# A hybrid decoder layer on one core: q and k of all gated-delta heads projected first, one triangular solve for twelve blocks, and the norm's row factor applied behind the projections

## The reference

```
h = rms_norm(x, norm_w)                      # x * rsqrt(mean(x*x) + eps) * norm_w
proj = h @ w_in                              # 2048 -> 4*(4+6+6)*128 + 12 columns
# 4 retention heads, 6 gated-delta heads, 6 block-attention heads, 128 wide
# gated-delta group, per head, in chunks:
q, k, v = silu(causal_conv4(proj_q)), silu(causal_conv4(proj_k)), silu(causal_conv4(proj_v))
q, k = l2_norm(q) * 128**-0.5, l2_norm(k)
g, beta = -exp(a_log) * softplus(a + dt_bias), sigmoid(b)
decay = exp(g_cum[i] - g_cum[j]);  m = strict_lower((k*beta) @ k.T * decay)
w, u = triangular_solve(m + I, [k*beta*exp(g_cum), v*beta])
v_new = u - w @ state;  o = (q*exp(g_cum)) @ state + (q @ k.T * decay) @ v_new
y = rms_norm(o, gdn_norm_w) * silu(z)
out = x + concat(y_ret, y_gdn, y_moba) @ w_out
```

## Time and profile before

| | before |
|---|---|
| median of 3 runs | 545.01 us (544.94 to 545.31) |
| profiled execution: time, span of its instructions | 544.99 us, 543.2 us |
| PE busy, PE weight loads | 529.7 us, 443.8 us |
| DVE, ACT, POOL busy | 326.8, 276.8, 47.4 us |
| granted TensorE clock over the span | 0.999 |
| chain that ended last | PE 96%, DMA 1%, ACT 1% |

### The profile page before, as it was taken

The page is one execution under the profiler, slowest core; times in us unless marked ns, Lnnn a source line. Parts: engine busy times, 40 slices in busy tenths (PEclk is TensorE's granted clock), DMA queues, the critical chain, the costliest instruction groups (busy, mean ns, idle before and its releaser), DMA issues.

```text
span 543.2 us, 8033 instructions
## 1 busy us (share of the span) xinstructions
PE 529.7 (98%) x3104; PEld 443.8 (82%) x3104; DVE 326.8 (60%) x548; ACT 276.8 (51%) x439; POOL 47.4 (9%) x49
## 2 busy tenths in 40 slices
PE   3999999999999999999999999999999999999997
PEld 3887888888888887788888888888888888888885
DVE  2776877768687877556454545366455445646451
ACT  4766664556455653446553554555366446543330
POOL 1003030212031021100100000010010001000000
PEclk9999999999999999999999999999999999999999
DMA  8997664546345653657567756765755666767811
GB/s 275 215 284 195 161 183 122 152 122 158 102 130 135 175 139 99 158 151 194 127 183 195 192 150 189 187 174 156 192 149 157 198 195 180 210 197 227 272 40 39
DMA packets 149929, 91.77 MB, mean 169 GB/s; under 512 B 7843, under 2 KB 139138, under 8 KB 149762
## 3 DMA queue, kind: packets, MB, share of 16 engines
q1 hardware_dynamic: 148562, 88.95, 60.7%
q10 hardware_dynamic: 1328, 2.31, 1.2%
HBM read 89.13 MB, written 2.10 MB: 168 GB/s over the span
## 4 chain that ended last, share of the span: by engine, by line
PE 96%; DMA 1%; ACT 1%; POOL 0%; issue 0%; DVE 0%; ACTq 0%
PE pj L1245 19%; PE pj L1243 19%; PE pj L1246 19%; PE pj L1221 13%; PE pj L1222 6%; PE pj L1287 3%; PE mx L1386 2%; PE mx L1376 2%; DMA cst<-table_dram 1%; PE pj L1292 1%; PE mx L1363 1%; PE pj L1218 1%; PE mx L1277 1%; PE mx L1270 1%; PE pj L1217 1%; PE mx L1460 1%
## 5 line engine op out<-in xcount | busy, mean ns | idle before, releaser
L292 DVE TENSOR_TENSOR w_lo<-w_raw,w_hi 128x1024 fp32r<-128x1024 f32 x160 | 194.6, 1225 | 90.9 <-ACT w_hi L374 90.7
L374 ACT ACTIVATE w_hi<-w_raw 128x1024 fp32r<-128x1024 f32 x160 | 169.1, 1058 | 152.1 <-PE pj L1246 136.4
L1243 PE MATMUL pj<-w_hi,hT 128*128 128x512 f32 x320 | 127.0, 397 | 0.0
L1245 PE MATMUL pj<-w_hi,hT 128*128 128x512 f32 x320 | 127.0, 397 | 0.0
L1246 PE MATMUL pj<-w_lo,hT 128*128 128x512 f32 x320 | 125.0, 391 | 0.0
L1221 PE MATMUL pj<-hT,w_hi 128*128 128x512 f32 x300 | 111.6, 408 | 0.0
L1222 PE MATMUL pj<-hT,w_lo 128*128 128x256 f32 x300 | 84.1, 280 | 0.0
L1246 PEld LDWEIGHTS pj<-w_lo,hT 128*128 128x128 f32 x320 | 60.1, 188 | 12.1
L1245 PEld LDWEIGHTS pj<-w_hi,hT 128*128 128x128 f32 x320 | 60.2, 188 | 12.0
L1243 PEld LDWEIGHTS pj<-w_hi,hT 128*128 128x128 f32 x320 | 60.1, 188 | 12.0
L1221 PEld LDWEIGHTS pj<-hT,w_hi 128*128 128x128 f32 x300 | 56.4, 188 | 12.0
(11 more groups left out here) (220 smaller groups left out, 487.5 us busy)
## 6 DMA issues: line engine op xcount, KB each, us to landing
w_raw<-in_w_in_dram SPq DMA_DIRECT2D x256, 256.0 KB, 3.4
w_raw<-in_w_out_dram SPq DMA_DIRECT2D x64, 256.0 KB, 4.0
big<-in_x_dram SPq DMA_DIRECT2D x8, 256.0 KB, 5.4
out_dram<-sq ACTq DMA_DIRECT2D x8, 256.0 KB, 4.1
big<-in_x_dram SPq DMA_DIRECT2D x1, 1024.0 KB, 4.9
big<-in_x_dram SPq DMA_DIRECT2D x2, 512.0 KB, 7.6
cst<-table_dram SPq DMA_DIRECT2D x1, 682.0 KB, 5.9
cst<-table_dram ACTq DMA_DIRECT2D x1, 196.0 KB, 7.4
```

What stands on the lines that cost most here:

```text
L292: eng.tensor_tensor(w_lo[:, n % NSPLIT, :], w_raw[:, n % NRAW, :], w_hi[:, n % NSPLIT, :].bitcast(F32), ALU.subtract).then_inc(S("lo"), 1)
L374: act.activation(w_hi[:, n % NSPLIT, :], w_raw[:, n % NRAW, :], ACT.Copy).then_inc(S("hi_done"), 1)
L1243: ins = pe.matmul(bank[:, :], src[:, kc, 0, tok], hi[:, k, :], start=first, stop=False)
L1245: pe.matmul(bank[:, :], src[:, kc, 1, tok], hi[:, k, :], start=False, stop=False)
```

## The change

1. **Start.** x is loaded in five column pieces of 2, 2, 4, 4 and 4 blocks, the pieces laid between the weight tiles in SP's queue. The identity alone (`cst[:, 0:P]`) is the first DMA of ACT's queue. x is transposed unscaled; group 0 needs the norm's weight but not its row factor. Squares are summed in quarters behind the blocks, the row factor is ready near the end of group 0, is spread by two transposes into `rb` (128 x 256), and multiplies the results: POOL's `add_halves` has a second operation per section, DVE multiplies the a/b rows, and ACT's copies of groups 6 to 15 take it as their scale. The small parameter DMAs move from SP's queue into ACT's.
2. **Order of columns.** `section(g, s)` makes groups 0 to 2 the q and k of heads pairs 0, 1, 2, and groups 3 to 5 their v and z.
3. **Solve.** `prepare(j)` (Gram, norms, decay, k rows) of the three pairs stands at units 110 to 262; then all 12 blocks are solved as one, 16 units a level; then `chain(p)` of the three pairs, 32 units each, ends before unit 512. Intermediates lie in the not yet written half of `yT` (`home`). The solve's matmuls are the same in number and shape.

```diff
-HALVES = [(0, 0), (2, HALF), (1, 0), (3, HALF), (0, HALF), (2, 0), (1, HALF), (3, 0)]
+HALVES = [(n + m, (a + m * HALF // GDN) % P) for a in (0, HALF) for n in range(GDN) for m in (0, GDN)]
...
+U_SUM, U_CUM = 74, 100
+U_ROWS = (110, 150, 200)
+U_PREP = (120, 176, 240)
+U_SOLVE = 262
+U_X = [U_SOLVE + 16 * _l for _l in range(LEVELS - 1)]
+U_Y = [_u + 7 for _u in U_X]
+U_VTOK, U_TURN = U_Y[3], U_Y[4] + 9
+U_X[5], U_Y[5] = U_TURN + 4, U_TURN + 11
+U_CHAIN = [U_Y[5] + 7 + 32 * _j for _j in range(GDN // 2)]
...
+        X_PIECES = [(0, 2), (2, 4), (4, 8), (8, 12), (12, 16)]
...
             for n in range(TILES):
                 load(n)
+                if n in (0, 1, 3, 5):
+                    load_piece(sp, (n + 1) // 2 + 1)
...
-            act.dma_start(cst[:, 0:K_FIRST], table[:, 0:K_FIRST]).then_inc(S("cst_in"), 16)
+            act.dma_start(cst[:, 0:P], table[:, 0:P]).then_inc(S("ident_in"), 16)
+            act.dma_start(prow[R_NORM:R_CONV, :], norm_w[0].rearrange("(k p) -> k p", p=P)).then_inc(S("ident_in"), 16)
...
-                pool.tensor_tensor(raw[:, g % 2, s, PAD:], ev[:, n % 2, 0:T], ev[:, n % 2, T:2 * T], ALU.add).then_inc(S("evac"), 1)
+                pool.tensor_tensor(ev[:, n % 2, 0:T], ev[:, n % 2, 0:T], ev[:, n % 2, T:2 * T], ALU.add).then_inc(S("halves"), 1)
+                if n == 0:
+                    pool.wait_ge(S("rb_done"), 1)
+                pool.wait_ge(S("halves"), n + 1)
+                pool.tensor_tensor(raw[:, g % 2, s, PAD:], ev[:, n % 2, 0:T], rb[:, :], ALU.mult).then_inc(S("evac"), 1)
...
-            pe.wait_ge(S("cst_in"), 16)
-            pe.wait_ge(S("norm_in"), 16)
+            pe.wait_ge(S("ident_in"), 2 * 16)
             pe.transpose(mx[3][:, 0:KC], prow[0:KC, :], ident[0:KC, 0:KC]).then_inc(S("norm_psum"), 1)
-            keep_busy(14)
-            pe.wait_ge(S("x0_scaled"), 1)
+            keep_busy(3)
             for b in range(2):
-                x_blocks(b, 0)
-            keep_busy(6)
-            pe.wait_ge(S("x1_scaled"), 1)
-            for b in range(2):
-                x_blocks(b, 1).then_inc(S("hT_psum"), 1)
-            keep_busy(8)
+                pe.wait_ge(S(f"x_in{b}"), 16 * C)
+                for c in range(C):
+                    ins = x_blocks(b, c)
+                ins.then_inc(S("hT_psum"), 1)
+                keep_busy(4)
...
+            pe.wait_ge(S("rstd_done"), 1)
+            for c in range(C):
+                pe.transpose(mx[3][:, c * P:(c + 1) * P], sm[:, 6 + c:7 + c].broadcast_to([P, P]), ident)
...
-            stream(68)
+            stream(U_SUM)
...
+            silu_kq(0, 0)
+            advance(106)
+            silu_kq(0, 1)
+            advance(112)
             decay_clip(0)
+            advance(116)
+            conv(1, 0, 0)
             decay_mask(0)
+            advance(122)
+            conv(1, 1, 0)
+            advance(128)
+            norms(0)
...
+            solve()
```

More of the change, by code:

```diff
@@ L303, in _ @@
         def _(sp):
[L304 to L307, removed]
+            load_piece(sp, 0)
             def load(n):
@@ L849, in _ @@
             dve.wait_ge(S("cst_in2"), 16)
-            for sec in range(3):
-                conv(0, 0, sec)
             steps = [0]
@@ L1020, in mix_gdn @@
+                    advance(U_X[l - 1] + 5)
                     if l == 1:
[L1021 to L1031 removed]
@@ new lines, in _ @@
+            conv(1, 1, 0)
+            advance(128)
+            norms(0)
+            advance(136)
+            conv(1, 0, 1)
+            advance(142)
+            lower(0)
+            scalars(0)
+            advance(148)
+            inverse_of_pairs(0)
+            queries(0)
+            advance(154)
+            conv(1, 1, 1)
+            decay_clip(1)
+            advance(160)
+            silu_kq(1, 0)
+            silu_kq(1, 1)
+            decay_mask(1)
+            advance(168)
+            conv(2, 0, 0)
@@ new lines, in _ @@
+            advance(176)
+            conv(2, 1, 0)
+            advance(184)
+            norms(1)
+            advance(192)
+            conv(2, 0, 1)
+            advance(200)
+            lower(1)
+            scalars(1)
+            advance(206)
+            inverse_of_pairs(1)
+            queries(1)
+            decay_clip(2)
+            advance(212)
+            conv(2, 1, 1)
+            silu_kq(2, 0)
+            advance(222)
+            silu_kq(2, 1)
+            decay_mask(2)
+            advance(236)
@@ new lines, in _ @@
+            norms(2)
+            advance(242)
+            lower(2)
+            inverse_of_pairs(2)
+            advance(248)
+            queries(2)
+            solve()
+            for p, (kind, j) in enumerate(PAIRS):
+                if kind == "gdn":
+                    chain(p)
+                else:
+                    if PAIRS[p - 1][0] == "gdn":
+                        mean_square(p - 1, True)
+                        norm_out(p - 1, True)
+                        advance(U_CHAIN[p - 1] + 38)
+                        gated_pair(p - 1, mx[2], [sm[:, 96 + RET:97 + RET]] * 2)
+                    {"ret": mix_ret, "moba": mix_moba}[kind](p, j, 128 * (p + 1))
@@ L1364, in mix_gdn @@
                                         start=True, stop=True)
                 ins.then_inc(S("gram"), 1)
+                pe.wait_ge(S("sq"), 2 * j + 2)
+                pe.wait_ge(S("clip_done"), 4 * j + 4)
+                for h in range(2):
+                    pe.transpose(mx[3][:, h * P:(h + 1) * P], kqs[:, j, h, 0, 0, :], ident)
+                for n in range(4):
+                    ins = pe.matmul(mx[3][:, 2 * P + n:2 * P + n + 1], sq[:, n // 2, n % 2, 1, :], ones[:, 0:1], start=True, stop=True)
@@ L1366, in mix_gdn, with v_tokens, solve @@
+                ins.then_inc(S("ktr"), 1)
+            def v_tokens(j):
+                pe.wait_ge(S("silu_v"), j + 1)
+                if j:
+                    pe.wait_ge(S("os"), j)
+                for n in range(4):
+                    ins = pe.transpose(mx[2][:, n * P:(n + 1) * P], vT[:, n // 2, (n % 2) * P:(n % 2 + 1) * P], ident)
+                ins.then_inc(S("vtok"), 1)
+            def solve():
                 for l in range(1, LEVELS):
-                    stream(U[f"x{l}"])
+                    stream(U_X[l - 1])
```

805 lines of the change are left out of this document (408 added, 397 removed).

## The result

The changed kernel takes 539.44 us in the median of four runs (537.86 to 540.47) against 544.98 (544.67 to 545.31): a ratio of 0.9898, 95% interval 0.9878 to 0.9917. Forecast were 535.3, with a range of 531 to 541.5. It is faster, inside the range, and 4.1 us short of the forecast.

The account below looks back on a forecast made before the run. PE bound the kernel, busy 529.7 of 543.2 us. From 544.99: -7.2 start, -0.6 a/b wait, +0.3 row-factor transposes, -7.0 merged batches, +3.6 DVE late, +1.2 POOL beside DVE, giving 535.3 us; range 531 to 541.5.

Parts of the forecast that it names:

- The start: Before group 0: PE starts earlier, group 0 begins at 8.3 instead of 15.49, gain 7.2 us; row-factor transposes later cost 0.3.
- about 6 us, before PE asks for them: Initial loads: identity, first x pieces and tile 0 arrive by about 6 us, so PE does not wait for x's second piece.
- double behind 3.4 us of transposes: Transposes before group 0: PE's pace doubles after 3.4 us of transposes alone, as read from the trace before.
- rival C: Start and first tile: transposes don't raise PE's pace, so group 0 begins slow, costing 2.3 us, 537.6 us; chance 0.12.
- The a/b wait: After group 0: PE's wait for the copy of the a/b rows goes, since ten units stand before the use; -0.6 us.
- The merged batches: Solve on PE: a 48-matmul batch costs 1.80 us, three of 16 cost 2.40; saving the fixed part gives -7.0 us.
- DVE late, and POOL beside it: Unit 64 to 262: DVE's list ends late, +3.6 us; twelve more POOL operations slow DVE, +1.2 us.
- Most are cheap: POOL beside DVE before unit 262: conv's mean lies just 17 ns above its median, so each added operation costs DVE 0.1 us.
- between nothing and 0.37: POOL beside DVE before unit 262: bounds in us of DVE's loss per added POOL operation, 0 to 4.4 us in all.
- the four places: Where PE stalls on DVE: decay rows 0.9, k rows of pair 0 0.5, Gram of pair 1 1.1, solve start 0.8 us.
- the distances between steps are those of before: Chains after the solve: step distances unchanged, so no waits or costs were counted there.
- rival D: Merged solve: DVE's widened steps make PE wait at each of twelve steps, slower than before, 550.9 us; chance 0.04.

Follow-up runs that it names:

- repaired: Changed kernel with dummy matmuls after x block 0 doubled, row-factor transposes after 4 gate-column matmuls, retention out batches 4 units later: 537.17 us, ratio 0.9853.
- start_only: Kernel before with only the change's new start, own order of heads and 16-matmul batches kept, no merged solve: 545.53 us, ratio 1.0011.
- low_parts_early: Changed kernel with DVE's low parts of tiles 9 and 10 done before its wait for the a/b projection: 539.86 us.
- taps_two: Changed kernel with one of DVE's three conv steps left out (18 conv steps fewer in the trace), POOL's work kept: 534.54 us.
- start_only_2: Kernel before with only the new start, no merged solve, decay-sum batch at unit 98 and first row batch at 106: 549.34 us.
- row_mult_twice: Changed kernel with each POOL multiply by the row factor made twice, 24 more POOL instructions, same results: 545.34 us, ratio 1.0005 to the kernel before.
- late_solve: Changed kernel with decay rows, preparation and solve placed 4 to 14 units later: 539.40 us.
- solve_in_thirds: Changed kernel with each of the twelve merged solve batches cut on PE into three parts, one stream unit apart: 546.33 us.
- no_row_mult: Changed kernel without POOL's 24 multiplies by the row factor (groups 0 to 5 left unscaled): 535.53 us, ratio 0.9829.
- start_only_3: Kernel before with only the new start, no merged solve, convs spread between gate steps, gate sums at unit 72, first rows at 102: 543.89 us, ratio 0.9984.

## Why the prediction was right or wrong

The forecast was a gain of 9.7 us, the measured one 5.5; the range held. Between the forecast and the profiled execution lie 5.2 us, 1.0 of which is this execution's distance from the median.

**The start** was the largest error in this execution: -6.9 forecast with the row factor's transposes, -4.5 measured at unit 64. Three steps failed. The first is the order of "about 6 us, before PE asks for them": x's second piece came after PE was ready, a gap of 0.66 us, and group 0 began at 8.89 and not 8.3.

The second is the pace. The prediction has it double behind 3.4 us of transposes; but the x block at 11.84 in the kernel before still ran at the slow one (1.06 us for four), and the distances halve at about 12.95, 4.4 us behind PE's first instruction. Here they halve at about 11.2, in the first tile, 7.4 us behind PE's first instruction, which costs 1.1. This is rival C, in part: the tile is slow, at half of its 2.3. What delays the doubling stays open. Counted from PE's first instruction it came after 4.0 us in *repaired*, with no gap, and after 7.4 and 7.5 with gaps of 0.66 and 0.82. But in between there is no order: a gap of 0.3 gave a first tile of 2.09 in *start_only*, 2.46 in *low_parts_early* and 2.95 in *taps_two*, and one of 0.6 gave 2.12 in *start_only_2* and 2.90 in *row_mult_twice*. One execution without a gap doesn't show that the gap is the cause. The rule that rival C named ("TensorE: Matmul & The Clock Gate", Part 4, of the Trainium skill) would have the first tile slow in either kernel; the fence of *repaired*, where the pace doubles among the transposes (0.60 us for the last four), speaks against it, as the earlier trace rows did.

The third was not foreseen at all: PE waits 0.6 us for the row factor. POOL's power takes 1.81 us where it takes 0.70 in *repaired*, *late_solve* and three more runs: it starts 0.02 us before a low part of DVE and stands still behind it. Nothing between 0.70 and 1.80 occurs in the eleven executions with this start, six long and five short, and only the long ones leave PE waiting, so this term too is a matter of chance.

**The a/b wait** went, as forecast: -0.65.

**The merged batches** were right in mechanism and near in size: -8.4 by the trace, -6.9 by *solve_in_thirds*, -7.0 forecast. A 48-batch cost 1.74, not 1.80. The fixed part of a batch is what merging saves, 0.29 to 0.35 us.

**DVE late, and POOL beside it**: +3.6 and +1.2 forecast, 4.8 together; to the start of the solve the three stalls cost 1.6, 1.6 and 1.5 between starts of PE, 4.7. But the split was wrong. Without the multiplies one stall of 1.1 is left there, so the load alone makes about 1, and the contention 3.9 and not 1.2. "Most are cheap" is the sentence that failed: a multiply cost DVE 0.29 us in the mean (7.0 / 24 by *no_row_mult*), not 0.1, near the upper end of the prediction's own "between nothing and 0.37". The earlier trace rows show the adds where DVE had slack, and the changed kernel has two POOL instructions per section where DVE has none. And of the four places two came (decay rows; Gram of pair 1), the k rows and the start of the solve did not, and a low part at 111.1 took the place of the latter. That the sum came out, 4.8 against 4.7, was luck.

**After the solve** nothing was counted ("the distances between steps are those of before"). The out transposes lost 2.6 us: where the batches of all eight pairs should take 0.45 us each, 3.6, they took 6.2. About half of that lies in the chains of the gated-delta heads (at 201.4 and at 231.1, with the wait of 0.7), half in the two retention pairs (0.4 of wait each). *repaired* gives the retention pairs 4 units more, and their two waits are gone; the one at the gated-delta chain it leaves as it was.

In the solve itself the 12-block steps of DVE took 0.95 to 0.98 us, as forecast, and PE waited for none: rival D had nothing. Adding up by the starts of PE: -4.5 for the start, -0.65 - 8.4 + 7.3 behind it (4.7 + 2.6), together -6.25 where the span fell by 4.8. That leaves some 1.5 us spread over the execution that I could not place, and 0.3 outside the span.

The net by parts, from medians: the start alone 1.1 (*start_only_3*), the merge 6.9 (*solve_in_thirds*), together 8.0, and the change gave 5.5. The 2.5 between them agree in size with the out transposes' 2.6, but no run isolates that, and the two parts were measured in kernels with different orders of columns.

## What to carry to other kernels

An engine with no waits in front of it makes each head start of the bottleneck a loan: ask, for every microsecond won early, whether the second engine can deliver that much earlier too. Small batches between the instructions of a saturated PE cost a fixed part each, so merge them, once the widened steps of the other engine fit the gaps. When an instruction is added to POOL, count what stands on DVE at that moment, not POOL's own idle time; here each cost DVE 0.29 us in the mean. And before two executions are compared, see whether their starts differ by chance: here one and the same start code put unit 64 anywhere between 37.9 and 39.8 us.

## What the runs showed of the hardware

**A POOL instruction waits for a whole DVE instruction.** Same stretch of the changed kernel, two engines in one timeline:

```profile
40.57 3.08 POOL L781 TENSOR_TENSOR ev<-ev 128x256 f32<-128x256 f32 x1
...
40.71 2.34 DVE L326 TENSOR_TENSOR w_lo<-w_raw,w_hi 128x1024 fp32r<-128x1024 f32 x2
```

3.08 is 0.74, the duration with DVE idle, and 2.34, both low parts. A power of four columns shows it too, with DVE idle and with a low part of 1.23 us that starts at 267.00:

```profile
229.07 1.01 POOL L754 TENSOR_TENSOR sm<-sm,cst 128x4 f32<-128x4 f32 x1 [7.47 <-DVE sm L974]
267.09 2.01 POOL L754 TENSOR_TENSOR sm<-sm,cst 128x4 f32<-128x4 f32 x1 [30.73 <-DVE sm L976]
```

So the two don't share a rate, one stands still, and DVE's conv steps of up to 1.02 us instead of 0.48 beside POOL are the same thing the other way round. Who goes first can turn on very little. The power of the row factor and a low part start 0.02 to 0.03 us apart in the changed kernel and in *late_solve*:

```profile
33.92 1.81 POOL L754 TENSOR_TENSOR sm<-sm,cst 128x2 f32<-128x2 f32 x1 [33.06 <-DVE sm L875]
33.94 1.22 DVE L326 TENSOR_TENSOR w_lo<-w_raw,w_hi 128x1024 fp32r<-128x1024 f32 x1
```

```profile
32.97 0.70 POOL L754 TENSOR_TENSOR sm<-sm,cst 128x2 f32<-128x2 f32 x1 [32.12 <-DVE sm L875]
33.00 1.25 DVE L326 TENSOR_TENSOR w_lo<-w_raw,w_hi 128x1024 fp32r<-128x1024 f32 x1
```

In the second the low part loses 0.03 us and the power nothing; in the first the power loses 1.1 and PE behind it 0.6. The recorded starts don't tell who goes first: POOL's is the earlier in both, and also in the add at 40.57 that waits, while an add at 75.81 holds up the low part at 75.85 (1.78 us instead of 1.22). The Trainium skill has this ("SBUF — State Buffer", "SBUF: two separate sides"): the two engines take turns at a port pair, held for the whole instruction, when DVE's has two SBUF inputs and POOL's reads SBUF. The rows in which POOL stands still agree with it; the last pair does not show the pair held for the whole 0.70, since the low part lost only 0.03.

**The granted clock fell behind some waits of PE and not behind others.** It read 0.50 to 0.52 behind waits of PE of 1.9 us (*row_mult_twice*, with one of 1.4 five microseconds earlier), 2.5, 2.6 and 3.8 us, for 3.5 us or, in the first case, 6.7. The fall came 0.2 to 1.7 us after PE had gone on. The clock stayed at 1.00 behind a wait of 1.9 in *late_solve* and behind the one of 2.6 in *row_mult_twice*. What tells the two sorts apart stays open. In such a stretch a unit takes 0.64 us instead of 0.35, so the wait of 2.6 in *start_only* cost 1.6 us more than itself: a late engine is priced too low if only its lateness is counted.
